# Second weight quarter loaded row by row, its first row's lower half made ahead of a norm: one hybrid-attention layer on one core

## The chip, the cores and the metric

The kernel runs on one core of a Trainium2 chip. Time is device time of one execution in microseconds (us), the median of three runs. The engines named below are TensorE (PE: matmuls; PEld in the profile is its weight load), VectorE (DVE), ScalarE (ACT), GpSimd (POOL) and SyncE (SP, which issues most transfers). An engine takes its own instructions in the order written; engines and transfers wait for each other by semaphores.

## The reference, cut to what matters

```python
h = rmsnorm(x, norm_pre_g)                  # x: 512 x 1024 fp32
u = einsum('bsd,de->bse', h, w_in)          # w_in: 1024 x 4096
# dq, dk, dv, dg, mq, mk, mv, mg = 8 pieces of 512 columns of u
# differential attention (4 heads) on dq, dk, dv; block attention (8 heads) on mq, mk, mv;
# T5 bias and causal mask in both; each output times silu of its gate columns (dg, mg)
y = einsum('bse,ed->bsd', concat(a_out, b_out), w_out)   # w_out: 1024 x 1024
out = x + rmsnorm(y, norm_post_g)
```

The change concerns only the start of the first product, `rmsnorm(x) @ w_in`.

## The kernel before

**Numbers as pairs.** Matmuls run in fp16. Each fp32 operand is split into an upper half `hi` (the value rounded to fp16) and a lower half `lo` (the rest), and a product is `hi*hi + hi*lo + lo*hi`. For weights ACT makes `w_hi` (lines 748, 749) and DVE makes `w_lo` (lines 910, 912 in `split`; line 899 in `split_row`, which does one row of a quarter). The norm's weight g goes into the weights.

**Tiles.** x has four tiles of 128 rows (t = 0 to 3). A group of weights is 1024 x 512 and comes as four quarters; a quarter is two "rows" k of 128 x 512 fp32 (256 KB each) and has one of four places in `stage`. Quarter n holds rows k = 2n and 2n+1 of group 0, which is the v columns. A unit is a 128 x 512 result over all eight k.

**The first unit is different.** So that PE can start early, unit 0 (tile 0) is computed in fp32 straight from `stage` (`first_quarter`, line 592; two passes for each k), with tile 0's norm applied afterwards. Behind its third quarter PE transposes tile 1 (line 539), which must have been normed by DVE (`x_norm(1)`, line 977). Units 1 to 3 (tiles 1 to 3) are `late_lower_unit`: first 16 matmuls that need only the upper half of the turned x tile (line 611), then 8 with its lower half (line 618).

**The norms.** For each tile t ACT squares one half of the columns (`x_square`, line 735), DVE squares the other (`x_half_square`, line 963), DVE adds the sums (`x_mean_square`, line 971), and POOL takes the power -0.5 (line 481, `x_rstd`). Tile 1's factor is waited for by DVE's `x_norm(1)`. Tile 2's and 3's are waited for by ACT's `xn_hi(2)`, `xn_hi(3)` (line 823), which make the normed upper half; SP then turns it by a DMA transpose (line 400), and PE's unit 2 or 3 starts when that has landed. Tile 1's upper half is made by ACT from PE's transposes (`x_hi(1)`, line 788), its lower half by DVE (`x_lo(1)`, line 1012).

**Order.** All order is written out by hand: the calls in each engine's block are the queue of that engine. SP issues x tile 0, quarter 0, x tile 1, then quarter 2, quarter 3, x tile 2 (this one after `w_loaded[1]`, the landing of quarter 1), x tile 3, and so on. Quarter 1 alone is issued from ACT's queue (line 833).

Of the kernel before, what the change touches and what calls it, by code (L numbers as in the profile page):

```python
# [7 lines left out]
def bass_hymba_diff_moba_layer(  # L8
# [26 lines left out]
    ACT = mybir.ActivationFunctionType  # L35
# [6 lines left out]
    WIDTH = SEQ  # L42
# [116 lines left out]
    w_in_v = w_in[0].rearrange("(k p) n -> p k n", p=P)  # L159
# [20 lines left out]
    with ctx:  # L180
# [3 lines left out]
        def sem(name):  # L184
            return ctx.enter_context(nc.semaphore(name))
# [94 lines left out]
        rows_stored = sem("rows_stored")  # L280
        strips_loaded = [sem(f"strips_loaded{r}") for r in range(2)]
        w_loaded = [sem(f"w_loaded{i}") for i in range(4)]
        xres_loaded = [sem(f"xres_loaded{t}") for t in range(TILES)]
        stored = [sem(f"stored{i}") for i in range(2)]
        stored_last = sem("stored_last")
# [249 lines left out]
        def _(pe):  # L535
# [50 lines left out]
            def first_quarter(q):  # L586

                pe.wait_ge(x_first_ready, q // 2 + 1)
                pe.wait_ge(w_loaded[q], 16)
                for k in (2 * q, 2 * q + 1):  # L590
                    cols = slice(k % 2 * WIDTH, (k % 2 + 1) * WIDTH)
                    last = nc.tensor.matmul(unit_ps[:, 0, :], x_first[:, k, :], stage[:, q, cols], start=(k == 0),  # L592
                                            stop=(k == KT - 1))
                last.then_inc(first_read if q < 3 else unit_done, 1)
# [132 lines left out]
        def _(act):  # L727
# [10 lines left out]
            def split(n):  # L738

                g, k = n // 4, 2 * (n % 4)  # L740
                act.wait_ge(w_loaded[n % 4], 16 * (n // 4 + 1))
                if g >= 3:
                    act.wait_ge(unit_done, LAST_OF_GROUP[g - 3] + 1)
                src = stage[:, n % 4, :].rearrange("p (k n) -> p k n", k=2)
                if g < len(GROUPS):
                    if n == 0:
                        act.wait_ge(g_scaled, 1)
                    nc.scalar.activation(w_hi[:, g % 3, k, :], src[:, 0, :], ACT.Copy, scale=g_cols[:, k:k + 1])  # L748
                    nc.scalar.activation(w_hi[:, g % 3, k + 1, :], src[:, 1, :], ACT.Copy,  # L749
                                         scale=g_cols[:, k + 1:k + 2]).then_inc(split_hi, 1)  # L750
                else:
                    nc.scalar.activation(w_hi[:, g % 3, k:k + 2, :], src, ACT.Copy,
                                         scale=W_SCALE).then_inc(split_hi, 1)
# [72 lines left out]
            def x_square(t):  # L826
# [3 lines left out]

            nc.scalar.dma_start(g_rows[:, :], norm_pre_g[0].rearrange("(k p) -> k p", p=P)).then_inc(gpre_loaded, 16)  # L831
            first = GROUPS[0][2]
            nc.scalar.dma_start(stage[:, 1, :].rearrange("p (k n) -> p k n", k=2),
                                w_in_v[:, 2:4, first:first + WIDTH]).then_inc(w_loaded[1], 16)
            x_square(0)
            split(0)
            x_square(1)
# [55 lines left out]
        def _(dve):  # L893
            def split_row(n, part):

                g, k = n // 4, 2 * (n % 4) + part
                dve.wait_ge(split_hi, n + 1)
                src = stage[:, n % 4, part * WIDTH:(part + 1) * WIDTH]
                ins = nc.vector.scalar_tensor_tensor(w_lo[:, g % 3, k, :], src, g_cols[:, k:k + 1],
                                                     w_hi[:, g % 3, k, :], ALU.mult, ALU.subtract)  # L900
                if part == 1:
                    ins.then_inc(split_lo, 1)
# [219 lines left out]
            split(0)  # L1122
            x_half_square(1)
            x_mean_square(1)
            x_norm(1)
            split(1)
            split_row(2, 0)
            x_half_square(2)
            x_mean_square(2)
            split_row(2, 1)  # L1130
            x_half_square(3)
            x_mean_square(3)
            split(3)
# [92 lines left out]
```

## Time and profile before

| | us |
|---|---|
| median of three runs (lowest, highest) | 253.86 (253.48, 253.91) |
| profiled execution | 253.41 |
| its span in the trace | 251.6 |
| PE busy | 244.8 (97%) |
| DVE busy | 178.4 (71%) |
| ACT busy | 142.9 (57%) |
| POOL busy | 30.1 (12%) |

Times in the trace count from the start of the span. A busy time on PE includes the matmul's tail, which overlaps the next one; the distance from start to start tells the pace. In a row of the timeline the square bracket gives how long the engine had stood idle before and what ended that. A landing is read as the issue's time plus the time "to landing".

### The profile page before, as it was taken

To read this page: it belongs to the slowest core of one execution; us is meant where nothing else is said; L and a number is where in the kernel's file an instruction comes from. 1 tells how busy PE (TensorE), PEld (TensorE's weight loads), DVE (VectorE), ACT (ScalarE), POOL (GpSimd) and SP (SyncE) were. 2 spreads that over 40 slices of the span, in tenths; PEclk is the share of its full clock that TensorE was granted. 3 is DMA by queue.
4 is the path that set the end of the run, shared out by engine and by line. 5 is a ranking of instruction groups with operands and counts; after the bars stand their busy time and mean duration, and the time that the engine had idled before them with its cause. 6 is when DMAs were issued, how large, how long until landed. Compare 5 with 4: busy or idle time off the path is not lost.

```text
span 251.6 us, 4449 instructions
## 1 busy us (share of the span) xinstructions
PE 244.8 (97%) x1564; PEld 122.5 (49%) x1564; DVE 178.4 (71%) x396; ACT 142.9 (57%) x336; POOL 30.1 (12%) x73
## 2 busy tenths in 40 slices
PE   8999999999999999999999999999999999999991
PEld 7444444445444554544455444454444444555570
DVE  3899786587477788868777767968788896835313
ACT  3894675274456666574676595577566655611110
POOL 1267000000000410040041032000000000111101
PEclk9999999999999999999999999999999999999998
DMA  7978989605765545443935553577749876982422
GB/s 262 389 225 188 315 261 375 193 5 135 107 182 141 181 115 145 139 157 106 208 96 137 147 161 112 131 199 179 179 102 199 202 182 155 198 208 42 125 86 83
DMA packets 59674, 42.47 MB, mean 169 GB/s; under 512 B 45808, under 2 KB 46072, under 8 KB 59652
## 3 DMA queue, kind: packets, MB, share of 16 engines
q1 hardware_dynamic: 59364, 41.66, 62.0%
q10 hardware_dynamic: 288, 0.53, 0.6%
q8 instruction: 13, 0.21, 0.4%
q14 instruction: 9, 0.07, 0.1%
HBM read 29.04 MB, written 2.13 MB: 124 GB/s over the span
## 4 chain that ended last, share of the span: by engine, by line
PE 94%; DMA 3%; issue 1%; DVE 0%; DVEq 0%; ACTq 0%; ACT 0%; POOLq 0%; POOL 0%
PE unit_ps L581 73%; PE score_ps L637 6%; PE o_ps L658 5%; PE unit_ps L611 4%; DMA stage<-in_w_in_dram 3%; PE unit_ps L592 2%; PE unit_ps L618 2%; PE unit_ps L712 1%; PE score_ps L712 1%; PE score_ps L539 0%; DVE area L1107 0%; DVEq L180 0%; ACTq L831 0%; ACT junk L735 0%; POOLq L180 0%
## 5 line engine op out<-in xcount | busy, mean ns | idle before, releaser
L581 PE MATMUL unit_ps<-area,w_hi 128*128 128x512 f16 x256 | 76.3, 380 | 0.0
L796 ACT ACTIVATE arena<-arena,negmax 128x512 f32<-128x512 f32 (+3 forms) x64 | 35.4, 554 | 50.0 <-DVE negmax L1034 49.9
L581 PE MATMUL unit_ps<-w_hi,area 128*128 128x512 f16 x192 | 60.3, 380 | 0.0
L581 PE MATMUL unit_ps<-area,w_lo 128*128 128x512 f16 x128 | 48.6, 379 | 0.0
L581 PEld LDWEIGHTS unit_ps<-area,w_hi 128*128 128x128 f16 x256 | 24.0, 98 | 27.3 <-issue 1.1
L581 PE MATMUL unit_ps<-w_lo,area 128*128 128x512 f16 x96 | 36.4, 379 | 0.0
L1034 DVE CUSTOM_DVE_ANT_0 arena<-score_ps,strips 128x512 f32<-128x512 f32 (+3 forms) x64 | 28.6, 485 | 9.4 <-PE score_ps L637 9.4
L910 DVE SCALAR_TENSOR_TENSOR w_lo<-stage,g_cols,w_hi 128x512 f16<-128x512 f32 x31 | 23.7, 765 | 10.1 <-ACT w_hi L749 10.1
L581 PEld LDWEIGHTS unit_ps<-w_hi,area 128*128 128x128 f16 x192 | 18.8, 98 | 21.9 <-issue 1.2
L748 ACT ACTIVATE w_hi<-stage,g_cols 128x512 f16<-128x512 f32 x32 | 22.7, 710 | 4.0 <-DMA stage<-in_w_in_dram 4.0
L912 DVE SCALAR_TENSOR_TENSOR w_lo<-stage,g_cols,w_hi 128x512 f16<-128x512 f32 x31 | 24.1, 778 | 0.0
L749 ACT ACTIVATE w_hi<-stage,g_cols 128x512 f16<-128x512 f32 x32 | 22.6, 707 | 0.0
L1063 DVE TENSOR_TENSOR arena<-arena 128x512 f16<-128x512 f32 (+5 forms) x32 | 21.0, 656 | 1.5 <-ACT arena L810 1.5
L810 ACT ACTIVATE arena<-arena 128x512 f16<-128x512 f32 (+5 forms) x32 | 19.0, 592 | 3.6 <-DVE arena L1054 3.5
L581 PE MATMUL unit_ps<-w_hi,q_hi 128*128 128x512 f16 x64 | 19.9, 380 | 0.0
L581 PEld LDWEIGHTS unit_ps<-area,w_lo 128*128 128x128 f16 x128 | 12.5, 98 | 15.1
L658 PE MATMUL o_ps<-v_hi,pt 128*128 128x64 f16 (+1 forms) x240 | 18.9, 202 | 0.0
L658 PEld LDWEIGHTS o_ps<-v_hi,pt 128*128 128x128 f16 x240 | 15.5, 98 | 3.8
L735 ACT ACTIVATE junk<-unit_ps 128x512 f16<-128x512 f32 (+1 forms) x8 | 4.5, 564 | 22.6 <-PE unit_ps L581 22.0
L658 PE MATMUL o_ps<-v_lo,pt 128*128 128x64 f16 (+1 forms) x120 | 16.2, 202 | 0.0
L581 PE MATMUL unit_ps<-w_hi,q_lo 128*128 128x512 f16 x48 | 14.9, 379 | 0.0
L503 POOL TENSOR_SCALAR sub_ms<-sub_sq 128x4 f32<-128x4 f32 x4 | 0.8, 193 | 113.2 <-ACT junk L735 113.2
(114 smaller groups left out, 356.7 us busy)
## 6 DMA issues: line engine op xcount, KB each, us to landing
stage<-in_w_in_dram SPq DMA_DIRECT2D x31, 512.0 KB, 4.0
stage<-in_w_out_dram SPq DMA_DIRECT2D x8, 512.0 KB, 4.2
arena<-in_x_dram SPq DMA_DIRECT2D x4, 512.0 KB, 5.0
strips<-bias_rows SPq DMA_DIRECT2D x4, 512.0 KB, 4.8
stage<-in_x_dram SPq DMA_DIRECT2D x4, 512.0 KB, 4.1
out_dram<-area SPq DMA_DIRECT2D x3, 512.0 KB, 2.7
strips<-bias_rows SPq DMA_DIRECT2D x1, 1024.0 KB, 8.0
stage<-in_w_in_dram ACTq DMA_DIRECT2D x1, 512.0 KB, 6.9
```

The lines of the kernel that those rows point to most:

```text
L581: last = nc.tensor.matmul(bank, a, b, start=(k == 0 and n == 0), stop=(k == KT - 1 and n == 2))
L611: nc.tensor.matmul(bank, ht[:, 0, k, rows], b[:, g % 3, k, :], start=(k == 0 and b is w_hi), stop=False)
L637: last = nc.tensor.matmul(score_ps[:, bank, col:col + n], a[part, ch, rows], b[part, ch, 0:n], start=first, stop=final)
L658: last = nc.tensor.matmul(o_ps[:, o % 2, col:col + width], a, b[:, k, src], start=(k == 0 and n == 0), stop=(k == t and n == 2))
L748: nc.scalar.activation(w_hi[:, g % 3, k, :], src[:, 0, :], ACT.Copy, scale=g_cols[:, k:k + 1])
L749: nc.scalar.activation(w_hi[:, g % 3, k + 1, :], src[:, 1, :], ACT.Copy, scale=g_cols[:, k + 1:k + 2]).then_inc(split_hi, 1)
L796: nc.scalar.activation(probs[:, i % 2, m, 0:n], probs[:, i % 2, m, 0:n], ACT.Exp, bias=negmax[:, i, m:m + 1], scale=-1.0, accum_out=sums[: ...
L810: nc.scalar.activation(hi, probs[:, i % 2, 0:1 + r, 0:n], ACT.Copy).then_inc(p_hi_ready, 1)
L910: nc.vector.scalar_tensor_tensor(w_lo[:, g % 3, k, :], src[:, 0, :], g_cols[:, k:k + 1], w_hi[:, g % 3, k, :], ALU.mult, ALU.subtract)
L912: nc.vector.scalar_tensor_tensor(w_lo[:, g % 3, k + 1, :], src[:, 1, :], g_cols[:, k + 1:k + 2], w_hi[:, g % 3, k + 1, :], ALU.mult, ALU.s ...
L1034: nc.vector.tensor_tensor_reduce(out=probs[:, i % 2, m, 0:n], in0=score_ps[:, bank, col:col + n], in1=strips[:, h, 0:n][:, ::-1], scale=-1 ...
L1063: nc.vector.tensor_tensor(lo, probs[:, i % 2, 0:1 + r, 0:n], hi, ALU.subtract)\
```

## The change

Quarter 1 comes in two transfers of one row each, both from ACT's queue, with a semaphore of its own for the first (`row_loaded`); `w_loaded[1]` is now raised by the second alone. PE waits for the row that it is about to read. ACT signals the first row's upper half by itself (`row_split`). DVE makes that row's lower half ahead of `x_norm(1)` and the second row's behind it. Quarter 2's lower half, of which one row stood behind `x_mean_square(2)`, is made in one piece before `x_half_square(2)`.

```diff
+        row_loaded = sem("row_loaded")
+        row_split = sem("row_split")
...
                 pe.wait_ge(x_first_ready, q // 2 + 1)
-                pe.wait_ge(w_loaded[q], 16)
                 for k in (2 * q, 2 * q + 1):
+                    pe.wait_ge(row_loaded if k == 2 else w_loaded[q], 16)
...
+                if n == 1:
+                    act.wait_ge(row_loaded, 16)
...
-                    nc.scalar.activation(w_hi[:, g % 3, k, :], src[:, 0, :], ACT.Copy, scale=g_cols[:, k:k + 1])
+                    row = nc.scalar.activation(w_hi[:, g % 3, k, :], src[:, 0, :], ACT.Copy,
+                                               scale=g_cols[:, k:k + 1])
+                    if n == 1:
+                        row.then_inc(row_split, 1)
...
-            nc.scalar.dma_start(stage[:, 1, :].rearrange("p (k n) -> p k n", k=2),
-                                w_in_v[:, 2:4, first:first + WIDTH]).then_inc(w_loaded[1], 16)
+            nc.scalar.dma_start(stage[:, 1, 0:WIDTH], w_in_v[:, 2, first:first + WIDTH]).then_inc(row_loaded, 16)
+            nc.scalar.dma_start(stage[:, 1, WIDTH:2 * WIDTH], w_in_v[:, 3, first:first + WIDTH])\
+                .then_inc(w_loaded[1], 16)
...
             def split_row(n, part):
...
-                dve.wait_ge(split_hi, n + 1)
+                if part == 0:
+                    dve.wait_ge(row_split, 1)
+                else:
+                    dve.wait_ge(split_hi, n + 1)
...
             x_mean_square(1)
+            split_row(1, 0)
             x_norm(1)
-            split(1)
-            split_row(2, 0)
+            split_row(1, 1)
+            split(2)
             x_half_square(2)
             x_mean_square(2)
-            split_row(2, 1)
             x_half_square(3)
```

DVE's queue before, from the mean square of tile 1 to that of tile 2. L971 is `x_mean_square`, L977 `x_norm(1)`, L910 and L912 the two rows of `split(1)`, L899 a row of quarter 2, L963 `x_half_square`:

```order
L971 TENSOR_TENSOR x_ms<-x_sq,x_half_sq 128x1 [waits x_half_squared,x_squared]
L977 TENSOR_SCALAR arena<-arena,x_rstd 128x1024 [waits x_rstd_ready]
L910 SCALAR_TENSOR_TENSOR w_lo<-stage,g_cols,w_hi 128x512 [waits split_hi]
L912 SCALAR_TENSOR_TENSOR w_lo<-stage,g_cols,w_hi 128x512
L899 SCALAR_TENSOR_TENSOR w_lo<-stage,g_cols,w_hi 128x512 [waits split_hi]
L963 ISA heads_out,x_half_sq<-arena 128x512 [waits x_half_squared,x_loaded2]
L963 ISA x_half_sq 128x1
L971 TENSOR_TENSOR x_ms<-x_sq,x_half_sq 128x1 [waits x_half_squared,x_squared]
L899 SCALAR_TENSOR_TENSOR w_lo<-stage,g_cols,w_hi 128x512 [waits split_hi]
L963 ISA heads_out,x_half_sq<-arena 128x512 [waits x_half_squared,x_loaded3]
```

The same stretch now; line numbers are those of the changed kernel (L982 mean square, L910 `split_row`, L988 `x_norm(1)`, L921 and L923 `split(2)`, L974 `x_half_square`):

```order
L982 TENSOR_TENSOR x_ms<-x_sq,x_half_sq 128x1 [waits x_half_squared,x_squared]
L910 SCALAR_TENSOR_TENSOR w_lo<-stage,g_cols,w_hi 128x512 [waits row_split]
L988 TENSOR_SCALAR arena<-arena,x_rstd 128x1024 [waits x_rstd_ready]
L910 SCALAR_TENSOR_TENSOR w_lo<-stage,g_cols,w_hi 128x512 [waits split_hi]
L921 SCALAR_TENSOR_TENSOR w_lo<-stage,g_cols,w_hi 128x512 [waits split_hi]
L923 SCALAR_TENSOR_TENSOR w_lo<-stage,g_cols,w_hi 128x512
L974 ISA heads_out,x_half_sq<-arena 128x512 [waits x_half_squared,x_loaded2]
L974 ISA x_half_sq 128x1
L982 TENSOR_TENSOR x_ms<-x_sq,x_half_sq 128x1 [waits x_half_squared,x_squared]
L974 ISA heads_out,x_half_sq<-arena 128x512 [waits x_half_squared,x_loaded3]
```

One row's split has moved from behind `x_norm(1)` to ahead of it, and one from between the mean square of tile 2 and the square of tile 3 to ahead of tile 2's square. The number of instructions is the same.

PE's queue before, from the first quarter of unit 0 to the transposes of tile 1 (L592 is `first_quarter`, one line for each k, L539 a transpose):

```order
L592 MATMUL unit_ps<-stage,gates 128x512 [waits w_loaded0,x_first_ready]
L592 MATMUL unit_ps<-stage,gates 128x512
L592 MATMUL unit_ps<-stage,gates 128x512 [waits w_loaded1,x_first_ready]
L592 MATMUL unit_ps<-stage,gates 128x512
L592 MATMUL unit_ps<-stage,gates 128x512 [waits w_loaded2,x_first_ready]
L592 MATMUL unit_ps<-stage,gates 128x512
L539 MATMUL score_ps<-ident,arena 128x128 [waits xs_ready]
```

And now:

```order
L594 MATMUL unit_ps<-stage,gates 128x512 [waits w_loaded0,x_first_ready]
L594 MATMUL unit_ps<-stage,gates 128x512 [waits w_loaded0]
L594 MATMUL unit_ps<-stage,gates 128x512 [waits row_loaded,x_first_ready]
L594 MATMUL unit_ps<-stage,gates 128x512 [waits w_loaded1]
L594 MATMUL unit_ps<-stage,gates 128x512 [waits w_loaded2,x_first_ready]
L594 MATMUL unit_ps<-stage,gates 128x512 [waits w_loaded2]
L541 MATMUL score_ps<-ident,arena 128x128 [waits xs_ready]
```

PE's order is the same; the third matmul waits for `row_loaded` in place of `w_loaded1`, and the fourth for `w_loaded1`.

## Rows read from the trace of the kernel before

**Rows 1.** The page: PE's busy time; the chain that ended last, by engine.
```profile
PE 244.8 (97%) x1564; PEld 122.5 (49%) x1564; DVE 178.4 (71%) x396; ACT 142.9 (57%) x336; POOL 30.1 (12%) x73
...
PE 94%; DMA 3%; issue 1%; DVE 0%; DVEq 0%; ACTq 0%; ACT 0%; POOLq 0%; POOL 0%
```
**Rows 2.** Waits, whole span: engine, line, who was waited for, us, times, longest.
```profile
PE unit_ps L592 <- DMA stage<-in_w_in_dram: 0.3, 1, 0.3
```
**Rows 3.** Chain of waits: start us, us, what.
```profile
1.34 6.94 DMA stage<-in_w_in_dram
```
**Rows 4.** Timeline of PE: start us, us, engine line op out<-in, count, idle before.
```profile
6.15 1.95 PE L592 MATMUL unit_ps<-stage,gates 128*128 128x512 f32 x4 [0.24 <-DVE gates L1001]
8.42 3.67 PE L592 MATMUL unit_ps<-stage,gates 128*128 128x512 f32 x8 [0.31 <-DMA stage<-in_w_in_dram]
11.93 1.04 PE L539 MATMUL score_ps<-ident,arena 128*128 128x128 f32 x8
...
14.63 0.38 PE L611 MATMUL unit_ps<-w_hi,area 128*128 128x512 f16 x1
...
18.08 1.89 PE L618 MATMUL unit_ps<-w_hi,area 128*128 128x512 f16 x8
19.81 0.38 PE L611 MATMUL unit_ps<-w_hi,area 128*128 128x512 f16 x1
```
**Rows 5.** Timeline of PE's weight loads, 14 to 15 us.
```profile
14.53 0.10 PEld L611 LDWEIGHTS unit_ps<-w_hi,area 128*128 128x128 f16 x1 [0.57 <-ACT area L788]
```
**Rows 6.** Timeline of ACT.
```profile
8.73 0.71 ACT L748 ACTIVATE w_hi<-stage,g_cols 128x512 f16<-128x512 f32 x1
...
12.85 0.63 ACT L735 ACTIVATE junk<-arena 128x512 f16<-128x512 f32 x1 [0.35 <-DMA arena<-in_x_dram]
...
13.47 1.00 ACT L788 ACTIVATE area<-score_ps 128x1024 f16<-128x1024 f32 x1
...
15.09 1.15 ACT L823 ACTIVATE pt<-arena,x_rstd 128x1024 f16<-128x1024 f32 x1
```
**Rows 7.** Timeline of DVE.
```profile
9.54 0.16 DVE L971 TENSOR_TENSOR x_ms<-x_sq,x_half_sq 128x1 f32<-128x1 f32 x1
10.37 0.76 DVE L977 TENSOR_SCALAR arena<-arena,x_rstd 128x1024 f32<-128x1024 f32 x1 [0.67 <-POOL x_rstd L481]
11.04 0.75 DVE L910 SCALAR_TENSOR_TENSOR w_lo<-stage,g_cols,w_hi 128x512 f16<-128x512 f32 x1
...
13.02 0.69 DVE L963 CUSTOM_DVE_ANT_0 heads_out<-arena 128x512 f32<-128x512 f32 x1
...
13.82 0.16 DVE L971 TENSOR_TENSOR x_ms<-x_sq,x_half_sq 128x1 f32<-128x1 f32 x1
13.90 0.74 DVE L899 SCALAR_TENSOR_TENSOR w_lo<-stage,g_cols,w_hi 128x512 f16<-128x512 f32 x1
...
15.44 0.75 DVE L910 SCALAR_TENSOR_TENSOR w_lo<-stage,g_cols,w_hi 128x512 f16<-128x512 f32 x1
...
16.76 1.22 DVE L1012 TENSOR_TENSOR area<-score_ps,area 128x1024 f16<-128x1024 f32 x1
```
**Rows 8.** Timeline of POOL.
```profile
6.27 0.56 POOL L481 TENSOR_TENSOR x_rstd<-x_ms,minus_half 128x1 f32<-128x1 f32 x1 [4.81 <-DVE x_ms L971]
...
9.78 0.55 POOL L481 TENSOR_TENSOR x_rstd<-x_ms,minus_half 128x1 f32<-128x1 f32 x1 [2.58 <-DVE x_ms L971]
14.06 0.99 POOL L481 TENSOR_TENSOR x_rstd<-x_ms,minus_half 128x1 f32<-128x1 f32 x1 [3.73 <-DVE x_ms L971]
15.60 0.99 POOL L481 TENSOR_TENSOR x_rstd<-x_ms,minus_half 128x1 f32<-128x1 f32 x1 [0.55 <-DVE x_ms L971]
```
**Rows 9.** Transfers issued from 4.2 to 4.4 us (quarter 2): count, size, us to landing.
```profile
stage<-in_w_in_dram SPq DMA_DIRECT2D x1, 512.0 KB, 5.3
```
**Rows 10.** Transposes issued from 16.2 to 16.4 us (tile 2's upper half).
```profile
area<-pt SPq DMA_TRANSPOSE x1, 3.2
```
**Rows 11.** Stretch 8.3 to 12.8 us: busy us of each engine (count), clock, DMA share, GB/s.
```profile
8.30:12.80 4.50, 4.38 (x17) 2.45 (x17) 3.72 (x8) 4.20 (x8) 0.55 (x1) 1.00 1.04 383
```

## The prediction, made before the changed kernel had run

> **What bounds the kernel now.** I read the page first: PE is busy for 97% of the span and makes up 94% of the chain that ended last [rows 1]. So the end moves only where PE stands still or is made to. The list of waits comes next: in the stretch that the change touches, PE waits for one transfer, 0.3 us, before the matmuls of line 592 [rows 2], and the chain names it: quarter 1, issued at 1.34, landed 6.94 later at 8.28 [rows 3]. PE's timeline then gives the true size. Eight matmuls from 8.42 to 11.93 go at 0.44 us each, so the four of quarter 0, started at 6.15, leave PE free at 7.91, and it starts again at 8.42 [rows 4]: a stall of 0.51 us, of which the bracket counts only 0.31 because the last matmul's tail is called busy. That is all that the first part of the change can win. Behind it I look for the next gates on PE, since a stall that goes is worth only what the nearest slack behind it leaves: unit 1 at 14.63, its lower part at 18.08, unit 2 at 19.81 [rows 4].
>
> **Part 1: quarter 1 in two transfers.** It adds one transfer issue on ACT's queue at the very start, where ACT has nothing to do until x tile 0 is there, so I take it at nothing; if it pushed anything it would be that landing, and no row speaks for it. The bytes and the queue's order stay. The first row is half of quarter 1 and must be there by 7.8. The trace does not show when half of the quarter was in: at an even flow it is midway between 1.34 and 8.28, at 4.8; at the worst it is 8.28 itself. I take a value before 7.8. The second row I take at 8.28 as before. PE then reads row 2 from 7.91 and row 3 from 8.79, when it is long there. Quarter 2 would start at 9.67; it was issued at 4.27 and landed 5.3 later, at 9.6 [rows 9], and PE needs 0.14 us from landing to matmul (8.28 to 8.42 [rows 3, 4]), so 9.7. Before, it was 8.42 + 4 x 0.44 = 10.18. Up to here PE has gained 0.47.
>
> **Part 2: the split ahead of the norm.** DVE stands idle for 0.67 us before the norm at 10.37, because it waits for POOL's power, and a row's split takes a slot of 0.66 (11.04 to 13.02 is three of them) [rows 7]. ACT's upper half of that row is made from 8.73 to 9.44 [rows 6], so DVE can start at 9.62 (0.08 after the mean square's start at 9.54, as 13.82 to 13.90 shows [rows 7]) and is free at 10.28. By DVE's own time the move fits into the hole and costs nothing.
>
> It does not fit for POOL. POOL's power took 0.55 and 0.56 us at 9.78 and 6.27, and 0.99 both times at 14.06 and 15.60 [rows 8]. At the first of these DVE was idle; at the two slow ones a split of 0.74 or 0.75 us had begun 0.16 us before, at 13.90 and 15.44 [rows 7]. The split reads both its large inputs, `stage` and `w_hi`, from SBUF. So a split that runs when POOL starts costs POOL 0.44 us: it gets going about 0.14 us before DVE's split ends. The changed kernel puts exactly such a split at 9.62, and POOL's power of tile 1 starts at 9.78, the same 0.16 later. It ends at 9.78 + 0.99 = 10.77 in place of 10.33, and the norm begins at 10.81 in place of 10.37.
>
> The Trainium skill states this in "SBUF — State Buffer", section "Who interferes with whom": a DVE instruction with two SBUF inputs contends with a GpSimd instruction that reads SBUF, and the one that comes second waits for the other. The trace agrees, with 0.99 against 0.55 us. By a reading in which the two engines are independent, the sum below would come to nothing instead of 0.2.
>
> The norm now ends at 11.56, so PE's transposes of tile 1 start at 11.66 (with 0.1 for the signal), not at 11.47 where PE would be ready; before it was 11.93. PE's gain shrinks to 0.27. Transposes, tile 0's factor and quarter 3 took 14.63 - 11.93 = 2.70, so PE is ready for unit 1 at 14.36.
>
> **The gate at unit 1.** Unit 1's first weights are what ACT makes at line 788, from 13.47 to 14.47; the weight load at 14.53 waited for it and the matmul followed at 14.63 [rows 5, 6]. The slack of this gate is nil. What sets ACT's 13.47 is not PE but x tile 2: ACT stood idle until 12.85 for its landing, squared it for 0.62, and then did line 788 [rows 6]. Tile 2 sits in SP's queue behind quarters 2 and 3, in a stretch in which the transfers' share is 1.04 [rows 11]; neither its place nor the bytes ahead of it change. So unit 1 starts at 14.63 as before, and the 0.27 left of the gain is given back here. Its lower part waits for DVE's line 1012, which ended at 17.98 for a matmul at 18.08 [rows 4, 7]; DVE has one split less between tile 2's mean square and it, which pays for the late norm: I get an end at about 17.8.
>
> **The gate at unit 2.** From the norm at 10.81 DVE has the same slots to tile 2's square as before (norm, three splits: 13.02 - 10.37 = 2.65), so that square starts at 13.46, not 13.02, and the mean square at 14.26 (13.02 to 13.82 is 0.80) [rows 7]. POOL starts 0.24 later, at 14.50 (13.82 to 14.06 [rows 7, 8]). What runs on DVE then is now tile 3's square (line 963, 0.69 us, from 14.34, both inputs from SBUF), in place of the split. If it holds POOL as a split does, POOL gets going at 14.34 + 0.69 - 0.14 = 14.89, and the factor is there at 15.44; before it was 15.05. If it does not, it is there at 15.05, exactly as before. No row shows POOL starting under a line 963; the nearest are the two at 0.99, and I take the hold. ACT's normed upper half of tile 2 (line 823, 15.09 before [rows 6]) then begins 0.39 late at 15.48 and ends at 16.62; the transpose lands 3.2 us after its issue [rows 10], at 19.85 in place of 19.46. PE wants unit 2 at 19.81 and needs 0.14 from landing to matmul: 19.99 against 19.81, a new stall of 0.18, up to 0.26 if the first matmul after a stall is again the longer one. I take 0.2.
>
> **The sum.** Stall at quarter 1: minus 0.51. Waiting again at quarter 2, at the transposes and before unit 1: plus 0.51. New stall before unit 2: plus 0.2. From there PE runs without a gap, and later steps keep their distance. The profiled execution took 253.41 us (span 251.6); this makes it 253.6. It lies 0.45 below the median of the runs shown, 253.86, so the forecast is 254.1 for the median. Bounds of the sum: minus 0.5 (all gates move along with PE) to plus 0.7 (the late factor and a late x tile 2 both).
>
> **Rivals.** *Nothing moves (253.9).* Tile 3's square does not hold POOL, so tile 2's factor comes at 15.05 as before, and only unit 1's gate acts. For it: a different kind of instruction, which reads the same tile twice. Against it: the operands lie in SBUF as the split's do.
>
> *The gain comes through (253.4 to 253.6).* If x tile 2 lands some 0.3 earlier, unit 1 can start when PE is ready, at 14.36, for 0.27; if POOL is also not held at tile 1, up to 0.5. For it: ACT has the 0.35 us of idle time before 12.85 to give. Against it: nothing in the edit speeds x tile 2, and unit 2's gate stands behind.
>
> *Slower by 0.6 (254.5).* The row transfers are served one after the other beside x tile 1, and the second lands later than 8.28. SP issues x tile 2 only then. While quarters 2 and 3 are still in the queue this is hidden; from the point at which they have nearly drained (about 10) tile 2 lands as much later, and with unit 1's slack at nil PE stands still for as long. With 0.6 for tile 2, the time is 254.5. For it: ACT's queue is the one transfer that took 6.9 us. Against it: it would need nearly 2 us of delay, and the second row is issued right behind the first, near 2 us. That the split rows don't help at all, because PE is held by row 3 all the same, would need that row after 8.65 and is part of this case.
>
> **How the numbers follow.** New stall at unit 2: 0.5. Nothing moves: 0.27. Gain comes through: 0.13. Slower by x tile 2 or by a longer hold of POOL: 0.10. A measurement can tell about 0.2% (0.5 us) from no change. The first two lie within; of the third, about 0.05 reaches beyond 0.5, of the fourth 0.08, and I add a little for what the edit may disturb that no row shows: faster 0.06, same 0.84, slower 0.10. The range 253.5 to 254.6 takes in both neighbours and most of the two outer cases.
>
> **What would show it.** Right: no idle time on PE before the third matmul of line 594; POOL's second power at 0.99; the norm at 10.8; the first weight load of unit 1 still at 14.5, waiting for ACT; tile 2's power late by 0.4; idle time of some 0.2 on PE before unit 2, ended by a transpose. Wrong: unit 1 before 14.5 (then x tile 2 came early), unit 2 at 19.8 with tile 2's power at 15.05 (then the square does not hold POOL), or ACT's wait for x tile 2 ending after 13.

## The result and the profile after

The changed kernel takes 255.07 us (median of 6 runs, 254.75 to 255.65), the kernel before, run beside it on the same chip, 253.69 (6 runs): a ratio of 1.0054, 95% interval 1.0039 to 1.0069. It is slower by 1.4 us, where the prediction's sum had 0.2. The two profiled executions differ by a little more: 255.21 against 253.41, and spans of 253.3 against 251.6. (The forecast of 254.1 counted from a median of 253.86.)

The page after, share of the span by engine, and then of the chain that ended last (for [rows 1]):

```profile
PE 245.2 (97%) x1564; PEld 122.6 (48%) x1564; DVE 178.3 (70%) x396; ACT 143.1 (56%) x336; POOL 32.6 (13%) x73
...
PE 92%; DMA 2%; issue 1%; DVE 1%; ACT 0%; POOL 0%; DVEq 0%; SPq 0%; POOLq 0%
```

PE's busy time grew by 0.4 only. So most of the 1.7 is holes in PE's work. The list of waits has the largest of them (for [rows 2]; in total, times, longest):

```profile
PE unit_ps L594 <- DMA stage<-in_w_in_dram: 1.7, 1, 1.7
```

It is a wait of the same line for a weight transfer as before, grown from 0.3 to 1.7. PE's timeline says which (for [rows 4]):

```profile
7.62 5.39 PE L594 MATMUL unit_ps<-stage,gates 128*128 128x512 f32 x12 [1.69 <-DMA stage<-in_w_in_dram]
13.09 1.09 PE L541 MATMUL score_ps<-ident,arena 128*128 128x128 f32 x8
...
16.03 0.39 PE L613 MATMUL unit_ps<-w_hi,area 128*128 128x512 f16 x1
...
19.49 1.89 PE L620 MATMUL unit_ps<-w_hi,area 128*128 128x512 f16 x8
21.50 0.38 PE L613 MATMUL unit_ps<-w_hi,area 128*128 128x512 f16 x1
```

It stands ahead of the first matmul, so it is quarter 0, which nobody edited. Behind it all twelve matmuls of quarters 0, 1 and 2 run in one piece: the stall in their middle, 0.51 us before, is gone. The chain of waits, from its start to unit 2, names what held PE (for [rows 3]; start, us, what):

```profile
1.17 6.32 DMA stage<-in_w_in_dram
...
8.14 0.71 ACT w_hi L756
...
9.55 0.75 DVE w_lo L923
10.29 0.60 DVE heads_out L974
...
11.25 1.00 POOL x_rstd L483
...
12.28 0.76 DVE arena L988
...
13.09 1.09 PE score_ps L541 x8
```

Quarter 0, issued at 1.17, landed 6.32 later, at 7.49; before it was 1.19 + 4.8 = 6.0. From there the chain runs over ACT's and DVE's split of quarter 0, tile 1's square, POOL's power and the norm to PE's transposes. No such chain existed before: PE came to the transposes last.

**The ledger on PE**, where each later stall is PE's start less the moment at which it would have been ready at the pace of before:

| place | before | after | adds |
|---|---|---|---|
| first matmul of quarter 0 | 6.15 | 7.62 | +1.47 |
| stall at quarter 1 | 0.51 | none | -0.51 |
| transposes of tile 1 (ready 12.87) | 11.93 | 13.09 | +0.2 |
| unit 1 (ready 13.09 + 2.70 = 15.79) | 14.63 | 16.03 | +0.24 |
| unit 2 (ready 19.49 + 1.73 = 21.22) | 19.81 | 21.50 | +0.28 |

The sum is 1.69 (21.50 - 19.81), and the span grew by 1.7: behind unit 2 nothing more is lost.

**The transfers.** Columns: stretch, its length, busy time (count) of PE, PEld, DVE, ACT, POOL, granted clock, share of the 16 DMA engines, GB/s. Two windows of before, in which quarter 0, quarter 1 and x tile 1 come in and quarters 2 and 3 are under way:

```profile
5.00:6.00 1.00, 0.91 (x9) 0.71 (x7) 0.64 (x2) 0.00 (x0) 0.00 (x0) 1.00 1.04 401
4.00:8.00 4.00, 3.76 (x18) 2.39 (x18) 3.01 (x8) 2.06 (x4) 0.84 (x2) 1.00 1.04 406
```

And the same of after:

```profile
5.00:6.00 1.00, 0.94 (x9) 0.75 (x7) 0.61 (x2) 0.03 (x1) 0.00 (x0) 1.00 0.81 182
4.00:8.00 4.00, 2.31 (x15) 2.04 (x16) 2.41 (x7) 1.21 (x3) 0.84 (x2) 1.00 0.94 326
```

The transfers run at 326 GB/s instead of 406, for one microsecond at 182 instead of 401. The loss of 80 GB/s over these 4 us is 320 KB, or 0.8 us at 406. In that one microsecond the rate falls to less than half while the transfer engines' busy share falls only from 1.04 to 0.81: the engines are for the most part not idle, what they carry takes longer. The rows of quarter 1 land at 7.30 and 9.42; the whole quarter landed at 8.28 [rows 3]. Quarter 2 lands at 10.77, before at 9.6 [rows 9]. On x tile 2 the delay acts twice, because SP issues it only after `w_loaded[1]`. Its issue in before:

```profile
8.30 0.34 SPq L404 DMA_DIRECT2D arena<-in_x_dram  x1
```

In after, and then the issue rows of quarter 0 and of x tile 2 with KB and us to landing (for [rows 9]):

```profile
9.43 0.34 SPq L406 DMA_DIRECT2D arena<-in_x_dram  x1
...
stage<-in_w_in_dram SPq DMA_DIRECT2D x1, 512.0 KB, 6.3
...
arena<-in_x_dram SPq DMA_DIRECT2D x1, 512.0 KB, 4.9
```

Each issue comes 0.01 or 0.02 after the landing of quarter 1's last byte. Tile 2 is issued 1.13 later and takes 4.9 in place of 4.5: it lands at 14.32, 1.5 after the 12.82 of before.

**The gate at unit 1.** ACT's timeline and the weight load (for [rows 5, 6]):

```profile
14.34 0.63 ACT L737 ACTIVATE junk<-arena 128x512 f16<-128x512 f32 x1 [0.81 <-DMA arena<-in_x_dram]
14.97 1.00 ACT L795 ACTIVATE area<-score_ps 128x1024 f16<-128x1024 f32 x1
17.01 1.15 ACT L830 ACTIVATE pt<-arena,x_rstd 128x1024 f16<-128x1024 f32 x1 [0.42 <-POOL x_rstd L483]
```

```profile
16.02 0.10 PEld L613 LDWEIGHTS unit_ps<-w_hi,area 128*128 128x128 f16 x1 [0.85 <-ACT area L795]
```

ACT waits until 14.34 for x tile 2, squares it and only then makes tile 1's upper half, for which PE's weight load waits: the gate of before, 1.5 us later. This gate is also the wait that ends last at unit 1: by PE's own pace the unit could have begun at 15.79 (the ledger), ACT's upper half ended at 15.97. (The chain above stays on PE at this point, since the tail of PE's last matmul still counts as busy.) The third row is new: ACT waits 0.42 for POOL's factor of tile 2. The rows of POOL and DVE behind that (for [rows 7, 8]):

```profile
11.25 0.99 POOL L483 TENSOR_TENSOR x_rstd<-x_ms,minus_half 128x1 f32<-128x1 f32 x1 [4.02 <-DVE x_ms L982]
15.97 1.94 POOL L483 TENSOR_TENSOR x_rstd<-x_ms,minus_half 128x1 f32<-128x1 f32 x2 [3.73 <-DVE x_ms L982]
```

```profile
11.01 0.16 DVE L982 TENSOR_TENSOR x_ms<-x_sq,x_half_sq 128x1 f32<-128x1 f32 x1
11.08 0.74 DVE L910 SCALAR_TENSOR_TENSOR w_lo<-stage,g_cols,w_hi 128x512 f16<-128x512 f32 x1
12.28 0.75 DVE L988 TENSOR_SCALAR arena<-arena,x_rstd 128x1024 f32<-128x1024 f32 x1 [0.45 <-POOL x_rstd L483]
15.73 0.16 DVE L982 TENSOR_TENSOR x_ms<-x_sq,x_half_sq 128x1 f32<-128x1 f32 x1
15.88 0.69 DVE L974 CUSTOM_DVE_ANT_0 heads_out<-arena 128x512 f32<-128x512 f32 x1
```

The split of 11.08 holds POOL's power, which takes 0.99, and the norm starts 1.27 after the mean square in place of 0.83. The square of 15.88 holds the next one: the row counts two powers in 1.94, and ACT's wait for the first of them ended at 17.01, so that one, begun at 15.97, took about 1.0.

### The profile page after: what moved, and what is told of

Same layout as the page of the kernel before. It is cut to its first block, busy times and chain, and to the rows that moved or that the text cites. A ratio compares the mean times of both kernels' runs of the same rounds, so it can differ in the third digit from the quotient of the medians.

```text
span 253.3 us, 4451 instructions
## 1 busy us (share of the span) xinstructions
PE 245.2 (97%) x1564; PEld 122.6 (48%) x1564; DVE 178.3 (70%) x396; ACT 143.1 (56%) x336; POOL 32.6 (13%) x73
## 4 chain that ended last, share of the span: by engine, by line
PE 92%; DMA 2%; issue 1%; DVE 1%; ACT 0%; POOL 0%; DVEq 0%; SPq 0%; POOLq 0%
PE unit_ps L583 72%; PE score_ps L639 6%; PE o_ps L660 5%; PE unit_ps L613 4%; DMA stage<-in_w_in_dram 2%; PE unit_ps L620 2%; PE unit_ps L714 1%; PE unit_ps L594 1%; PE score_ps L714 1%; PE score_ps L541 0%; POOL x_rstd L483 0%; DVE arena L988 0%; DVE area L1118 0%; DVE w_lo L923 0%; ACT w_hi L756 0%
## 5 line engine op out<-in xcount | busy, mean ns | idle before, releaser
L921 DVE SCALAR_TENSOR_TENSOR w_lo<-stage,g_cols,w_hi 128x512 f16<-128x512 f32 x31 | 23.4, 755 | 11.2 <-ACT w_hi L756 11.1
L923 DVE SCALAR_TENSOR_TENSOR w_lo<-stage,g_cols,w_hi 128x512 f16<-128x512 f32 x31 | 24.1, 778 | 0.0
L660 PE MATMUL o_ps<-v_lo,pt 128*128 128x64 f16 (+1 forms) x120 | 16.2, 202 | 0.0
```

Source lines behind the costliest of these rows:

```text
L660: last = nc.tensor.matmul(o_ps[:, o % 2, col:col + width], a, b[:, k, src], start=(k == 0 and n == 0), stop=(k == t and n == 2))
L921: nc.vector.scalar_tensor_tensor(w_lo[:, g % 3, k, :], src[:, 0, :], g_cols[:, k:k + 1], w_hi[:, g % 3, k, :], ALU.mult, ALU.subtract)
L923: nc.vector.scalar_tensor_tensor(w_lo[:, g % 3, k + 1, :], src[:, 1, :], g_cols[:, k + 1:k + 2], w_hi[:, g % 3, k + 1, :], ALU.mult, ALU.s ...
```

## The experiments

Each is compared with the kernel before, run beside it on the same chip (medians 253.65 to 253.76 of 17 to 23 runs). The diffs are against it unless said otherwise.

### Which half of the change costs

**e1: the transfers alone.** The two row transfers and the waits for them; DVE's old order.

```diff
-            nc.scalar.dma_start(stage[:, 1, :].rearrange("p (k n) -> p k n", k=2), w_in_v[:, 2:4, ...]).then_inc(w_loaded[1], 16)
+            nc.scalar.dma_start(stage[:, 1, 0:WIDTH], w_in_v[:, 2, ...]).then_inc(row_loaded, 16)
+            nc.scalar.dma_start(stage[:, 1, WIDTH:2 * WIDTH], w_in_v[:, 3, ...]).then_inc(w_loaded[1], 16)
```

> The kernel before with quarter 1 in two row transfers (and the waits for them) alone; DVE's order is that of before. Theory T (the transfers are what costs): quarter 0 lands near 7.5 us as in the changed kernel, not at 6.0, PE's first fp32 matmul starts near 7.6, and the time is 1.0 to 1.4 us over before, about 254.8. Theory D (DVE's order and POOL's hold are what costs, the late landing is chance): quarter 0 lands near 6.0 and the time is within 0.2 us of before, about 253.6.

Measured: 254.45 us, ratio 1.0027 (1.0016 to 1.0037). Quarter 0 landed at 6.89, x tile 2 at 13.54. Its window:

```profile
4.00:8.00 4.00, 3.78 (x17) 3.14 (x18) 2.41 (x7) 1.81 (x4) 0.84 (x2) 1.00 0.99 347
```

The throughput falls and the other transfers come late with no edit on DVE. Unit 2 began at 20.65, 0.84 after that of before, without a stall of its own (18.91 + 1.73 = 20.64). The chain of waits says by which way:

```profile
1.74 7.12 DMA stage<-in_w_in_dram
...
8.87 4.66 DMA arena<-in_x_dram
...
14.29 0.92 ACT area L795
...
15.25 3.63 PE unit_ps L613 x16
```

The second row of quarter 1 lands at 8.86, SP issues x tile 2 at 8.87, and ACT's upper half of tile 1 and PE's unit 1 follow. Unit 1 begins 0.62 late (15.25 against 14.63), and its lower part another 0.2 (18.91 - 15.25 = 3.66, before 3.45). Quarter 0, 0.9 late, is not in this chain: PE was at the transposes at 12.25 and would have been ready for unit 1 at 12.25 + 2.70 = 14.95.

**e2: DVE's order alone.** One transfer for quarter 1; ACT's signal for the first row's upper half comes with it.

```diff
+            split_row(1, 0)
             x_norm(1)
-            split(1)
-            split_row(2, 0)
+            split_row(1, 1)
+            split(2)
             x_half_square(2)
             x_mean_square(2)
-            split_row(2, 1)
```

> The kernel before with DVE's new order alone (a row of quarter 1 split ahead of tile 1's norm, quarter 2 in one piece ahead of tile 2's square); quarter 1 is one transfer. Theory T: quarter 0 lands near 6.0 as before; POOL's powers of tiles 1 and 2 take 0.99 us each, tile 2's factor comes 0.4 late, PE stands still about 0.2 to 0.3 us before unit 2, and the time is 0.2 to 0.3 over before, about 253.95. Theory D: the time is over 1 us above before, about 255.

Measured: 253.96 us, ratio 1.0008 (0.9998 to 1.0018): not to be told from no change. Its windows, DVE and POOL rows:

```profile
4.00:8.00 4.00, 4.00 (x17) 3.21 (x18) 2.64 (x8) 2.06 (x4) 0.84 (x2) 1.00 1.04 405
...
11.08 0.75 DVE L984 TENSOR_SCALAR arena<-arena,x_rstd 128x1024 f32<-128x1024 f32 x1 [0.45 <-POOL x_rstd L482]
...
10.06 0.99 POOL L482 TENSOR_TENSOR x_rstd<-x_ms,minus_half 128x1 f32<-128x1 f32 x1 [2.24 <-DVE x_ms L978]
14.77 1.94 POOL L482 TENSOR_TENSOR x_rstd<-x_ms,minus_half 128x1 f32<-128x1 f32 x2 [3.73 <-DVE x_ms L978]
```

And PE's at tile 1's transposes and at unit 2:

```profile
11.98 1.04 PE L540 MATMUL score_ps<-ident,arena 128*128 128x128 f32 x8
...
18.16 1.90 PE L619 MATMUL unit_ps<-w_hi,area 128*128 128x512 f16 x8
20.25 0.38 PE L612 MATMUL unit_ps<-w_hi,area 128*128 128x512 f16 x1 [0.19 <-issue]
```

With the throughput whole, both holds of POOL are there, and unit 2 starts 20.25 - (18.16 + 1.73) = 0.36 late. So this step of the forecast is real, 0.36 us where 0.2 was forecast. The held power of tile 1 was not on PE's path in e2: the norm ended at 11.08 + 0.75 = 11.83, and PE came to the transposes only at 11.98. Parts and whole: 0.27% + 0.08% is 0.35%, with about 0.14 either way, against 0.54% (0.39 to 0.69). They agree within their uncertainty, so it is open whether the two make each other worse. The trace of after suggests it: there the chain from quarter 0's landing passes through the held power.

**e12: the same without a split ahead of the norm.**

```diff
             x_norm(1)
             split(1)
-            split_row(2, 0)
+            split(2)
             x_half_square(2)
             x_mean_square(2)
-            split_row(2, 1)
```

> The kernel before with quarter 2's split in one piece ahead of tile 2's square, and nothing moved ahead of tile 1's norm; quarter 1 is one transfer. Against e2 this takes away the split that runs while POOL makes tile 1's factor. If POOL is held by a running instruction of DVE with two SBUF inputs: its power of tile 1 takes 0.55 us again (0.99 in e2), the norm starts 0.83 after the mean square's start (1.27 in e2), and tile 2's power, started under tile 3's square, still takes 0.99. DVE has one split more (0.66) between norm and tile 2's square than before, so tile 2's factor comes 0.6 late and PE stands still 0.3 to 0.5 us before unit 2: time 0.3 to 0.4 over before, about 254.1. If the long power in e2 had another cause, it is 0.99 here too.

Measured: 254.25 us, ratio 1.0032 (1.0016 to 1.0047). POOL, then DVE:

```profile
10.06 0.55 POOL L481 TENSOR_TENSOR x_rstd<-x_ms,minus_half 128x1 f32<-128x1 f32 x1 [2.23 <-DVE x_ms L971]
15.00 1.94 POOL L481 TENSOR_TENSOR x_rstd<-x_ms,minus_half 128x1 f32<-128x1 f32 x2 [4.39 <-DVE x_ms L971]
...
10.64 0.75 DVE L977 TENSOR_SCALAR arena<-arena,x_rstd 128x1024 f32<-128x1024 f32 x1 [0.67 <-POOL x_rstd L481]
```

The first power is free again (0.55) and the norm comes 0.44 earlier than in e2, and unit 2 has the same stall (20.49 against 18.38 + 1.73: 0.38). The time is not better than that of e2; but e12 isn't e2 less the hold alone, since DVE has one split more between the norm and tile 2's square, and unit 1's lower part began 0.24 late too (18.38 - 14.69 = 3.69, before 3.45; in e2 3.48). What e12 shows is that the other move costs by itself: quarter 2's second row ahead of tile 2's square, which makes tile 2's mean square late and puts POOL under tile 3's square.

### What slows the transfers

**e3: quarter 0 in two rows as well** (e1 and this):

```diff
-            load_quarter(0)
+            sp.dma_start(stage[:, 0, 0:WIDTH], w_in_v[:, 0, ...]).then_inc(row0_loaded, 16)
+            sp.dma_start(stage[:, 0, WIDTH:2 * WIDTH], w_in_v[:, 1, ...]).then_inc(w_loaded[0], 16)
```

> As e1, and quarter 0 comes in two row transfers as well, on SP's queue. Theory M (the loss is a meeting: a row transfer walks the partitions twice as fast per byte as the two-row transfer of quarter 0 and catches up with it near 5 to 6 us, where both then read and write the same partitions): with both by rows they walk at one pace and never meet, throughput stays near 400 GB/s from 5 to 6.5 us, quarter 0's second row lands by 6.2, and the time is near before, about 253.7. Theory N (each further, smaller transfer costs by itself): three more transfer pieces than before, quarter 0 lands at 7.5 or later, time 254.8 or more.

Measured: 255.71 us, ratio 1.0076 (1.0060 to 1.0091), the slowest but one. Quarter 0's second row landed at 8.40. The idea that a row transfer meets a transfer of another order in the same memory, and that equal orders would cure it, falls as I had put it.

```profile
4.00:8.00 4.00, 3.55 (x16) 2.53 (x16) 2.41 (x7) 0.72 (x2) 0.84 (x2) 1.00 0.96 317
```

**e4 and e10: another source.** In e4 both rows of quarter 1 are read from `w_out` (the kernel then leaves out quarter 1's right weights); in e10 quarter 0 is too (leaves out those of quarters 0 and 1). The diff is against e1.

```diff
-            nc.scalar.dma_start(stage[:, 1, 0:WIDTH], w_in_v[:, 2, ...]).then_inc(row_loaded, 16)
+            nc.scalar.dma_start(stage[:, 1, 0:WIDTH], w_out_v[:, 2, 0:WIDTH]).then_inc(row_loaded, 16)
...
-                    src = w_in_v[:, k:k + 2, col:col + WIDTH]
+                    src = w_in_v[:, k:k + 2, col:col + WIDTH] if n else w_out_v[:, 0:2, 0:WIDTH]
```

> As e1, but the two row transfers of quarter 1 read w_out (rows 4 KB apart) in place of w_in (rows 16 KB apart); destination, size and order are the same. It leaves out quarter 1's weights of the first product. If the loss lies on the reading side (two transfers reading w_in a fixed distance apart), quarter 0 lands near 6.0 and the time is near 253.7; if it lies in the queues or on the writing side, quarter 0 lands near 7.5 as in e1 and the time is near 254.8.

> As e1, but quarter 0 and both rows of quarter 1 read w_out (rows 4 KB apart) in place of w_in (16 KB apart): it leaves out the right weights of these two quarters. If the loss is on the reading side and comes from the rows' distance, throughput from 4 to 7 us stays near 400 GB/s, quarter 0 lands near 6.0, and the time is near 253.7. If it is not, quarter 0 lands near 7 and the time is near 254.4.

Measured: 254.49 (ratio 1.0029, 1.0019 to 1.0040) and 254.52 (1.0040, 1.0025 to 1.0055). Quarter 0 landed at 6.80 and 7.43, with 344 and 356 GB/s, and the times are that of e1 (254.45): neither the distance between the sources nor the tensor makes the loss.

**e5 and e6: one queue.** Quarter 1 is issued from SP between quarter 0 and x tile 1, in e5 as two rows, in e6 whole.

```diff
             load_quarter(0)
+            load_quarter(1)        # e6; in e5 the two row transfers stand here
             load_x(1)
...
-            nc.scalar.dma_start(stage[:, 1, :] ...
```

> As e1 (quarter 1 in two row transfers, DVE's order of before), but both are issued from SP's queue between quarter 0 and x tile 1, so that no two of the first transfers share the queue's turn. Theory Q (the loss comes from row transfers in one queue running beside transfers of the other): quarter 0 lands before 5.6 us, throughput stays near 400 GB/s from 5 to 7 us, quarter 1 is in by 7, PE's stall at quarter 1 is gone, unit 1 still waits for x tile 2, time near before, 253.5 to 253.8. Theory N (each smaller transfer costs by itself, whatever the queue): throughput falls as in e1, x tile 2 lands 0.7 us late, time near 254.4.

> The kernel before with quarter 1 as one transfer, issued from SP between quarter 0 and x tile 1; nothing else changed. The control of the run with rows on one queue: quarter 0 lands before 5.6, quarter 1 by 7, no stall of PE at quarter 1. If x tile 2 still lands near 12.8, unit 1 starts at 14.6 as before and the time is 253.7 +- 0.2 (the stall that the change was after is worth nothing). If tile 2 comes earlier with it, up to 0.3 less, 253.4.

Measured: 254.31 (ratio 1.0026, 1.0011 to 1.0042) and 254.15 (1.0015, 1.0002 to 1.0028). In a single queue quarter 0 lands early (5.45 and 5.37), yet the throughput is low even with a whole quarter; here is e6:

```profile
4.00:8.00 4.00, 3.54 (x18) 2.04 (x17) 3.57 (x9) 2.06 (x4) 0.84 (x2) 1.00 0.98 355
```

In these executions the loss needs neither two queues nor the cut into rows. Quarter 1 was expected by 7 in e6 and landed at 8.03, and PE stood still before it after all, for 0.43. In both, x tile 2 was issued early (7.98 and 8.05) and still came at 13.2, unit 2 started 0.6 to 0.7 late (18.67 and 18.81 + 1.73), and a new wait for a turned x tile stands behind it, here of e6:

```profile
PE unit_ps L619 <- DMA area<-pt: 0.4, 1, 0.4
```

**e7: the quarter cut by partitions**, 64 and 64, both halves on ACT's queue; all wait for both.

```diff
+            for h in range(2):
+                half = slice(64 * h, 64 * h + 64)
+                nc.scalar.dma_start(stage[half, 1, :] ..., w_in_v[half, 2:4, ...]).then_inc(w_loaded[1] if h else row_loaded, 16)
```

> Quarter 1 in two transfers on ACT's queue, but cut by partitions (64 and 64, both rows in each), and PE waits for both; DVE's order of before. If two transfers behind each other on ACT's queue are what costs (theory N or Q), quarter 0 lands near 7 and the time is near 254.4 as in e1. If the cut by rows is what costs, quarter 0 lands near 6 and the time is near 253.8.

Measured: 258.42 us, by far the worst. Its six runs spread from 256.34 to 260.45; the ratio, 1.0154 (1.0122 to 1.0185), is that of the four shorter ones, up to 258.52. The profiled one was the longest, so its rows tell in what way the kernel can lose, not how much. The throughput of 4 to 8 us was 279 GB/s, and PE waited for quarter 1 (a row of PE's timeline, then two windows; the last three columns are clock, share and GB/s):

```profile
12.68 6.10 PE L596 MATMUL unit_ps<-stage,gates 128*128 128x512 f32 x8 [4.84 <-DMA stage<-in_w_in_dram]
...
9.00:10.00 1.00, 0.00 (x0) 0.00 (x0) 0.00 (x0) 0.00 (x0) 0.00 (x0) 1.00 1.13 188
...
13.00:14.00 1.00, 1.00 (x2) 0.48 (x2) 0.76 (x2) 1.00 (x3) 0.00 (x0) 0.50 0.73 215
```

PE stood idle from 7.83, and in that wait its granted clock fell from 1.00 to 0.50, 1.2 in place of 2.4 GHz. The eight matmuls behind it then took 6.10 us in place of 3.67 [rows 4]. So a good part of this execution's loss is the clock, on top of the late transfer. Whether the shorter executions had this too, no profile shows.

**e8: one row on each queue**, row 2 from ACT, row 3 from SP behind x tile 1. The diff is against e1 and shows the added issue; that of row 3 from ACT is gone.

```diff
             load_x(1)
+            sp.dma_start(stage[:, 1, WIDTH:2 * WIDTH], w_in_v[:, 3, ...]).then_inc(w_loaded[1], 16)
```

> Quarter 1 by rows, the first on ACT's queue, the second on SP's behind x tile 1; DVE's order of before. If the second transfer behind the first on ACT's queue is what costs, throughput from 5 to 6.5 us is whole again, quarter 0 lands near 6.0, row 3 near 8.5, and the time is 253.7 to 253.9. If the first row transfer beside quarter 0 is what costs, quarter 0 lands near 7 as in e1 and the time is near 254.4.

Measured: 254.55 us, ratio 1.0043 (1.0026 to 1.0060), 335 GB/s, quarter 0 at 7.11. A second transfer right behind the first in ACT's queue is not the cause either.

**e9 and e11: the same issues, later.** A small activation, waited for, ahead of ACT's issue moves it from 1.34 to 2.98: e9 with the two rows, e11 with the whole quarter.

```diff
+            nc.scalar.activation(late_sb[:, :], one_rows, ACT.Square).then_inc(late, 1)
+            act.wait_ge(late, 1)
```

> As e1 (quarter 1 in two row transfers on ACT's queue, DVE's order of before), but ACT issues them about 1.9 us later, behind a small activation. Theory M (row transfers catch up with quarter 0's while both are under way): quarter 0 is nearly through when row 2 begins, so it lands by 6.0, throughput from 5 to 6 us is 380 GB/s or more, row 2 lands by 7.2, row 3 by 8.8, and the time is 253.5 to 253.9. If two transfers where there was one cost by themselves, throughput falls to 200 to 300 GB/s all the same, only later, and the time is 254.3 or more.

> The kernel before with quarter 1 in one transfer, issued about 1.9 us later from ACT's queue, as a control of the late rows. Quarter 0 lands earlier than before, by 5.5; quarter 1 later, 8.5 to 9. If any change of when quarter 1 starts loses throughput, it falls below 350 GB/s from 5 to 6 us here too, and the time is 254 or more; if only row transfers lose it, it stays near 400 and the time is near 253.8 (the stall at quarter 1 some 0.3 longer, hidden behind x tile 2).

Measured: e9 253.82 (ratio 1.0013, 1.0000 to 1.0027), quarter 0 at 5.42; e11 254.43 (1.0029, 1.0019 to 1.0039), quarter 0 at 5.39. With quarter 0 ahead by itself it lands on time and the row version nearly reaches the kernel before. The throughput stays low all the same, 332 and 354; here is e11, which has only the transfer of before, issued 1.6 us later:

```profile
4.00:8.00 4.00, 3.90 (x17) 3.11 (x18) 2.64 (x8) 2.32 (x5) 0.84 (x2) 1.00 0.99 354
```

**All together** (landings in us, each from one profile; GB/s of 4 to 8 us):

| arrangement of quarter 1 | GB/s | quarter 0 | x tile 2 issued | x tile 2 landed |
|---|---|---|---|---|
| whole, ACT at 1.34: before, e2, e12 | 406, 405, 408 | 6.0, 5.80, 6.12 | 8.30, 8.18, 8.20 | 12.82, 12.61, 12.73 |
| two rows, ACT at 1.34: after, e1, e4, e10 | 326, 347, 344, 356 | 7.49, 6.89, 6.80, 7.43 | 9.43, 8.87, 9.11, 9.53 | 14.32, 13.54, 13.66, 13.49 |
| rows on two queues: e8 | 335 | 7.11 | 8.98 | 13.89 |
| SP alone: e5, e6 | 326, 355 | 5.45, 5.37 | 7.98, 8.05 | 13.19, 13.21 |
| ACT at 2.98: e9, e11 | 332, 354 | 5.42, 5.39 | 9.24, 9.07 | 13.20, 12.98 |

Three profiles of one arrangement lie at 405 to 408; the other nine of the table, e3 (317) and e7 (279) lie at 356 or below. For quarter 1 in two rows beside the old issues (after, e1, e4, e8) that loss is shown: the profiled executions lie within 0.4 us of their medians, and the intervals of all four lie above 1. For one queue and for the later issue it is weaker. The profiled executions of e5, e6, e9 and e11 took 254.71, 254.78, 254.61 and 254.68 us, against medians of 254.31, 254.15, 253.82 and 254.43, and those of e6 and e11 were the longest of all their runs; the shortest of e5 and e6 (253.24 and 253.17) were as fast as the fastest of the kernel before (253.27). That of e10 was its longest too. So that every execution of these kernels loses throughput isn't shown; it may be that some do and some don't. These kernels also ran on other chips than e2 and e12, of which two of the three whole profiles are. e11 is slower than before by 0.29% (0.19 to 0.39), with an edit of the moment alone, and that no spread explains.

Why the arrangement of before keeps its throughput, no run shows: that stays open.

## Why the prediction was wrong

**The failed step** is in part 1: "The bytes and the queue's order stay", and with it the silent assumption that transfers nobody edits keep their landings. The bytes did stay; the rate did not. I priced the second issue by what it does to ACT, which is nothing, and bounded only the first row of quarter 1. Two terms failed by it. "The second row I take at 8.28 as before": it landed at 9.42, and at 8.86 in e1. SP issues x tile 2 behind it, so tile 2 came 1.5 us late and with it unit 1, 1.40 late (16.03 against 14.63); with 0.01 before the unit's lower part and the 0.28 at unit 2 that is the whole 1.69. And quarter 0's landing was not among the bounds at all, though PE's first matmul of unit 0 can't begin ahead of it. That term, taken at zero, measured +1.47 at that matmul in after (quarter 0 at 7.49), and quarter 0 landed 0.8 to 1.5 us later than in before in all four kernels with this arrangement; by itself it would have made unit 1 1.16 late (15.79). The first row's landing ("before 7.8") came at 7.30. A window that I had read [rows 11], though a later one (8.3 to 12.8 us), should have warned me: there, as from 4 to 8 us, the transfers' share was 1.04, so a loss of rate had nothing spare to hide in.

**The stall at quarter 1** went, all 0.51 of it, but not in the way that was forecast: PE began the twelve matmuls 1.47 later, when the first row had long landed, and the second landed at 9.42, when PE was at quarter 1's first row. The same happened in e2 with one whole transfer: PE began quarter 0 at 6.73, ran twelve matmuls without a stall, and was at the transposes at 11.98, against 11.93 before. A late start only filled the stall. No run removed the stall with quarter 0 on time and the throughput whole. So what it is worth isn't measured, nor whether its gain would be given back at unit 1.

**POOL under the split**: forecast 0.99, measured 0.99 in after and e2, 0.55 in e12 without it. The rule of the Trainium skill weighed there ("SBUF — State Buffer", section "Who interferes with whom") holds in these traces. The time of the norm, 10.81 in the forecast, was 11.08 in e2, where POOL's power began 0.28 late (10.06 against 9.78) behind PE's slower transposes of tile 0, and 12.28 in after, where quarter 0's delay comes on top. In e2 the norm was not on PE's path; in after PE's transposes waited for it, with POOL's 1.00 us in the chain of waits, though unit 1 behind them then waited longer for ACT.

**The gate at unit 1**: the mechanism is as forecast (ACT's line 795 behind x tile 2), the place of tile 2 is not. In e2 and e12, where the throughput is kept, unit 1 began at 14.68 and 14.69, against a forecast 14.63, but not by this gate. x tile 2 was a little earlier there, and ACT's upper half of tile 1 was ready in e2 at 14.26:

```profile
13.26 1.00 ACT L792 ACTIVATE area<-score_ps 128x1024 f16<-128x1024 f32 x1
```

PE came to the unit by its own pace (11.98 + 2.70 = 14.68). In after unit 1 began at 16.03, behind ACT. "Neither its place nor the bytes ahead of it change" is true; it landed 1.5 us later, 1.13 of that by its later issue (9.43 against 8.30) and 0.4 by a longer way from there.

**The stall at unit 2**: forecast 0.2, measured 0.28 in after, 0.36 in e2. Tile 3's square does hold POOL: the one thing here that no row of before could show, and the nearest row (0.99) gave it well.

**The rival "slower by 0.6"** came nearest and got 0.10. Its chain is in the trace of after as described: the second row lands late, SP issues x tile 2 only then, and unit 1 moves with it. In e1, with the transfers alone, it is the chain of waits itself, and its price of 254.5 us is e1's time, 254.45. I dismissed it because a delay below "nearly 2 us" would be hidden while quarters 2 and 3 were in the queue. The row landed 1.14 late and it was not hidden, since those two quarters were late as well (quarter 3 at 12.07, before 10.91). The issue is only a part of it, though: e6 issued x tile 2 at 8.05, earlier than before, and had it 0.4 late; e11 issued it at 9.07 and had it 0.2 late. No run took SP's wait away, so how much of the 1.4 us hangs on it is not measured. What the rival left out is quarter 0. By PE's ledger the start alone was 1.47 late; but with x tile 2 at 14.32 unit 1 would have begun at 16.03 even with quarter 0 on time. The two delays overlap and can't be added, and the one behind x tile 2 ended last. Both transfers were in flight in the same microseconds of low rate.

## What to carry to other kernels

Where transfers run at full share in a stretch that the critical path depends on, an edit of one (cut, other queue, other moment) is to be priced on all that are in flight with it: on the one that is needed first, and on the one behind whose landing the next is issued. Bound it by at least the microsecond seen here, and measure it alone before any work is reordered around it. A stall of the busiest engine may be worth nothing until the next gate moves too; find which transfer sets that gate.

## What was unexpected of the hardware

- The flow of the first transfers depends on how they are issued: 405 to 408 GB/s in the three profiles of one arrangement, 279 to 356 in one profile each of eleven kernels with another. The Trainium skill says in "DMA: Bandwidth & Descriptors", section "Issuing engines are not separate DMA queues", that issuing from several engines only saves time on the issuing queue. e6, with all on one queue, measured 0.15% (0.02 to 0.28) more time than the kernel before, and 355 GB/s against 406 in its longest execution. It also puts quarter 1 ahead of x tile 1, so it does not decide whether the second queue does more than the page says.
- Cutting a 512 KB transfer by partitions (e7) costs 1.5% of the kernel's time, by rows (e1) 0.3%. In the one profile of e7 the granted clock fell to 0.50 while PE stood idle for 4.84 us, and matmuls that took 3.67 us before took 6.10 behind it: here a late transfer cost more than its wait.
- A squaring instruction of DVE that takes the same tile as both inputs holds POOL's power as a split with two different inputs does: about 1.0 us in after for the power begun under it (15.97 to ACT's start at 17.01), against 0.55 for a free one.
- The eight transposes of tile 0 on PE took 1.77 us in e1 and 1.69 in e2, at a granted clock of 1.00; tile 1's eight took 1.04 in both. In e2 it held back quarter 0's first matmul (6.73, landed 5.80) and cost next to nothing at the transposes of tile 1 (11.98 against 11.93), since it filled the stall at quarter 1. No run was made on its cause.
